# A two-column product of zeros ahead of a weight panel's run, and a dilated attention whose norm follows its first panel

## The reference

```python
def rms_norm(x, g):
    return x * lax.rsqrt(jnp.mean(x * x, axis=-1, keepdims=True) + EPS) * g

def swiglu(h, w_gate_up, w_down):                       # d_ff 2816
    gate, up = jnp.split(h @ w_gate_up, 2, axis=-1)
    return (jax.nn.silu(gate) * up) @ w_down

def first_block(x, ...):
    for i in range(4):                                  # fourier, s5, dilated, fourier
        x = x + mixer[i](rms_norm(x, norm_mix_g[i]))
        x = x + swiglu(rms_norm(x, norm_ffn_g[i]), ffn_w_gate_up[i], ffn_w_down[i])

def dilated_attention_mixer(h, w_qkv, q_gain, k_gain, w_o, rel_bias):
    qkv = (h @ w_qkv).reshape(b, s, 3, 3, 16, 64)       # 3 groups, (q, k, v), 16 heads
    for g, (window, dil) in enumerate(DILATED_GROUPS):
        q = head_rms_norm(qkv[:, :, g, 0], q_gain[g])   # t * rsqrt(mean(t * t) + EPS) * gain
        k = head_rms_norm(qkv[:, :, g, 1], k_gain[g])
        o, l = dilated_group_attention(q, k, qkv[:, :, g, 2], ...)
    ...                                                 # softmax over groups by l, then @ w_o

def second_block(x, ...):
    for i in range(2):
        h = h + 0.5 * swiglu_ffn(rmsnorm(h, norm_ffn1[i]), ...)
        u = rmsnorm(h, norm_mix[i]) @ w_mix_in[i]
        z, xbc, dt, q, k, v, q_idx, k_idx, w_idx = jnp.split(u, SPLIT_POINTS, axis=-1)
        h = h + jnp.concatenate([ssd_mixer(z, xbc, dt, ...), dsa_mixer(q, k, v, ...)], axis=-1) @ w_mix_out[i]
        h = h + 0.5 * swiglu_ffn(rmsnorm(h, norm_ffn2[i]), ...)
    return rmsnorm(h, final_norm)
```

## Time and profile before

| | |
|---|---|
| median of three executions | 2635.28 us |
| the profiled execution, own time | 2638.81 us |
| its span, first to last instruction | 2637.0 us |
| mean granted clock of TensorE | 0.982 |
| PE, PEld, DVE, ACT, POOL busy | 96%, 94%, 68%, 47%, 8% |
| products of panels | 18528, 48 for each of 386 panels |
| read from HBM | 426.45 MB, 162 GB/s over the span |

### The profile page before, as it was taken

The page is one execution under the profiler, slowest core; times in us unless marked ns, Lnnn a source line. Parts: engine busy times, 40 slices in busy tenths (PEclk is TensorE's granted clock), DMA queues, the critical chain, the costliest instruction groups (busy, mean ns, idle before and its releaser), DMA issues.

```text
span 2637.0 us, 54521 instructions
## 1 busy us (share of the span) xinstructions
PE 2526.9 (96%) x23166; PEld 2469.3 (94%) x23166; DVE 1783.4 (68%) x2299; ACT 1251.6 (47%) x1468; POOL 213.4 (8%) x246
## 2 busy tenths in 40 slices
PE   8999669999999899999999999999999999999998
PEld 7999669998999889999999999999999998999998
DVE  5988956565555665656666568976566557986655
ACT  5444434334566553344344346565334335665433
POOL 5000240003000100000000000600000000320000
PEclk9999889999999899999999999999999999999999
DMA  5553024555677735534545544434555554434553
GB/s 211 192 189 109 18 82 174 179 188 173 176 173 174 172 129 179 187 135 177 189 171 196 188 159 160 145 134 173 181 188 178 189 190 149 150 137 154 182 183 120
DMA packets 65839, 430.76 MB, mean 163 GB/s; under 512 B 8288, under 2 KB 11360, under 8 KB 15904
## 3 DMA queue, kind: packets, MB, share of 16 engines
q1 hardware_dynamic: 58864, 410.30, 43.3%
q0 software_dynamic: 6000, 17.46, 4.6%
q10 hardware_dynamic: 832, 0.92, 0.1%
HBM read 426.45 MB, written 1.15 MB: 162 GB/s over the span
## 4 chain that ended last, share of the span: by engine, by line
PE 88%; DVE 7%; ACT 3%; issue 1%; DMA 0%; DVEq 0%; ACTq 0%
PE psum L1989 26%; PE psum L1991 26%; PE psum L1990 26%; DVE w_lo L1313 1%; ACT w_hi L841 1%; PE psum L2022 1%; PE psum L2185 1%; PE psum L2091 1%; PE psum L2332 1%; PE psum L2320 1%; PE psum L2310 1%; PE psum L2276 0%; DVE h L1346 0%; PE psum L2074 0%; DVE rstd L1338 0%
## 5 line engine op out<-in xcount | busy, mean ns | idle before, releaser
L1989 PE MATMUL psum<-h_hi,w_hi 128*128 128x256 f32 x4320 | 1220.0, 282 | 20.9 <-DVE h_lo L1351 15.0
L1991 PE MATMUL psum<-h_hi,w_lo 128*128 128x256 f32 x4320 | 1211.2, 280 | 0.0
L1990 PE MATMUL psum<-h_lo,w_hi 128*128 128x256 f32 x4320 | 1210.6, 280 | 0.0
L841 ACT ACTIVATE w_hi<-raw 128x2048 fp32r<-128x2048 f32 x387 | 740.7, 1914 | 885.2 <-PE psum L1991 885.2
L1313 DVE TENSOR_TENSOR w_lo<-raw,w_hi 128x2048 fp32r<-128x2048 f32 x387 | 886.5, 2291 | 392.6 <-ACT w_hi L841 392.4
L1989 PEld LDWEIGHTS psum<-h_hi,w_hi 128*128 128x128 f32 x4320 | 814.8, 189 | 30.4 <-issue 25.7
L1990 PEld LDWEIGHTS psum<-h_lo,w_hi 128*128 128x128 f32 x4320 | 816.0, 189 | 0.7 <-issue 0.5
L1991 PEld LDWEIGHTS psum<-h_hi,w_lo 128*128 128x128 f32 x4320 | 815.5, 189 | 0.0
L1989 PE MATMUL psum<-act_hi,w_hi 128*128 128x256 f32 x1536 | 430.0, 280 | 0.7 <-DVE act_lo L1869 0.7
L1991 PE MATMUL psum<-act_hi,w_lo 128*128 128x256 f32 x1536 | 429.3, 280 | 0.0
L1990 PE MATMUL psum<-act_lo,w_hi 128*128 128x256 f32 x1536 | 428.9, 279 | 0.0
(11 more groups left out here) (329 smaller groups left out, 2374.3 us busy)
## 6 DMA issues: line engine op xcount, KB each, us to landing
raw<-in_panels SPq DMA_DIRECT2D x387, 1024.0 KB, 4.8
arena<-bias_by_distance POOLq DMA_DIRECT2D x32, 384.0 KB, 6.4
x<-in_x SPq DMA_DIRECT2D x1, 1024.0 KB, 5.7
arena<-in_s_cbd POOLq DMA_DIRECT2D x4, 256.0 KB, 3.0
arena<-in_s_b SPq DMA_DIRECT2D x1, 1024.0 KB, 15.2
arena<-in_s_c SPq DMA_DIRECT2D x1, 1024.0 KB, 17.1
hidden<-in_s_cbd POOLq DMA_DIRECT2D x4, 256.0 KB, 3.0
arena<-arena POOLq DMA_DIRECT2D x32, 32.0 KB, 1.9
```

Of the source, the lines that this page charges most:

```text
L841: a.activation(w_hi[:, s, :], raw[:, s, :], ACT.Copy).then_inc(hi_ready, 1)
L1989: t.matmul(o, w[0], xin[0], start=start, stop=False, skip_group_check=True)
L1990: t.matmul(o, w[0], xin[1], start=False, stop=False, skip_group_check=True)
L1991: return t.matmul(o, w[1], xin[0], start=False, stop=stop, skip_group_check=True)
```

## The change

It does three things.

The first is a new function, `lead`: one fp32 product of a 128 by 128 tile of zeros by two of its columns, into the first two columns of the bank that the coming panel clears as it starts. It stands behind the panel's wait for `lo_ready` and ahead of its first product. It is called 97 times: in the eight FFNs ahead of panel 1; in the two fourier mixers and in the S5 mixer ahead of the second panel; 32 times in dilated attention, ahead of each panel that stands behind another product; and 27 times in each mixer of the second network.

```diff
+            def lead(o, start=True):
+                z = zeros[:, :].bitcast(F32)
+                t.matmul(o[:, 0:2], z, z[:, 0:2], start=start, stop=True, skip_group_check=True)
...
-            def project(n, j, i=None, per=0, parts=None, o=None, frees=False):
+            def project(n, j, i=None, per=0, parts=None, o=None, frees=False, led=False):
...
+                    if led and k + m == 0:
+                        lead(o)
...
-                project(n0 + 1, 1)
+                project(n0 + 1, 1, led=True)
...
-            def project_tokens(n, o, tokens):
+            def project_tokens(n, o, tokens, led=False):
                 t.wait_ge(lo_ready, n + 1)
+                if led:
+                    lead(o)
...
+                def inner(p):
+                    return p >= 0 and 2 <= da_panel(p)[1] <= QK + 1
...
-                def arrive(p):
+                def arrive(p, led=False):
...
+                    led = p == Z + 3 or p == V + 1 or len(UNITS_AFTER[p - 1]) > 0
```

```diff
-            st["late"] = kind == "norm" and todo[len(stages) + 1][0] == "ffn"
+            st["late"] = kind == "norm" and todo[len(stages) + 1][0] in ("ffn", "dilated")
+            st["cols"] = kind == "norm" and todo[len(stages) + 1][0] == "dilated"
...
-                        a.activation(da.v[:, hb % 2, i - QK], b[:, :].rearrange("p (m n) -> p m n", m=2),
-                                     ACT.Copy).then_inc(v_copied, 1)
+                        for m in range(2):
+                            ins = a.activation(da.v[:, hb % 2, i - QK, m], b[:, m * S:(m + 1) * S], ACT.Copy,
+                                               scale=da.rstd[:, m:m + 1])
+                        ins.then_inc(v_copied, 1)
...
+                        if c == 0:
+                            a.wait_ge(rstd_ready, st["hn"] + 1)
+                        for qt in range(2):
+                            ins = a.activation(rq[:, :, qt], ss_q[:, :, qt], ACT.Sqrt, bias=da.eps[:, 0, qt:qt + 1])
+                        ins.then_inc(qk_rms_ready, 1)
...
+                if st["cols"]:
+                    for w, e in enumerate((E * EPS, EPS)):
+                        v.tensor_scalar(da.eps[:, w], bank[SUMS_BANK[True]][:, 0:2], e / D, e * EPS, ALU.mult, ALU.add)
+                    v.reciprocal(da.rstd, da.rstd).then_inc(rstd_ready, 1)
+                    return
...
-                t.wait_ge(rms_ready, st["hn"] + 1)
-                t.wait_ge(e_loaded, 16 * 5)
                 for p in range(PANELS):
-                    panel(p)
+                    panel(p, p == 1 or inner(p - 1))
+                    if p == 0:
+                        t.wait_ge(sq_added, 3 * (st["hn"] - st["whole"]))
+                        for qt in range(2):
+                            last = t.matmul(bank[SUMS_BANK[True]][:, qt:qt + 1], h[:, 0, qt::2], ones[:, 0:1],
+                                            start=True, stop=True)
+                        last.then_inc(ss_ready, 1)
+                t.wait_ge(rstd_ready, st["hn"] + 1)
```

More of the change, by code:

```diff
@@ L459, in build @@
         da.rk = da.take(2 * UNITS).rearrange("p (b n) -> p b n", b=2)
-        da.take(2 * 2 * S - 2 * UNITS)
+        da.rstd = da.take(2)
+        da.eps = da.take(2 * 2).rearrange("p (w t) -> p w t", w=2)
+        da.take(2 * 2 * S - 2 * UNITS - 6)
         da.rq = da.take(2 * NG * UNITS).rearrange("p (b g m t e) -> p b g m t e", b=2, g=NG, m=2, t=2)
@@ L873, in norm @@
                 a.wait_ge(ss_ready, n + 1)
-                a.activation(rstd[:, :], bank[SUMS_BANK[st["late"]]][:, 0:S], ACT.Sqrt, bias=eps[:, 0:1],
+                root, sums = (da.rstd, slice(0, 2)) if st["cols"] else (rstd[:, :], slice(0, S))
+                a.activation(root, bank[SUMS_BANK[st["late"]]][:, sums], ACT.Sqrt, bias=eps[:, 0:1],
                              scale=1.0 / D).then_inc(rms_ready, 1)
@@ L2279, in widen, with panel @@
                     last.then_inc(qk_wide_ready, 1)
-                def panel(p):
+                def inner(p):
+                    return p >= 0 and 2 <= da_panel(p)[1] <= QK + 1
+                def panel(p, led):
                     hb, i, _ = da_panel(p)
@@ L2340, in output @@
                     t.wait_ge(o_lo_ready, (tiles[-1] + 2) // 2)
+                    if k == 0 and tiles[0]:
+                        lead(bank[k], False)
                     for c in tiles:
@@ L2356, in dilated_mixer @@
                         scores(u)
-                    for p in da_panels(u):
-                        panel(p)
+                    for k, p in enumerate(da_panels(u)):
+                        panel(p, k == 0 or inner(p - 1))
                     if u and u % 2 == 0:
@@ L2384, in arrive, with accumulate @@
                     if p >= V:
-                        project_tokens(n0 + p, bank[p % PROJ_BANKS], (slice(0, P), slice(P, S)))
+                        project_tokens(n0 + p, bank[p % PROJ_BANKS], (slice(0, P), slice(P, S)), led=led)
                     else:
-                        project(n0 + p, p, parts=(h_lo_ready, 4 * st["hs"]) if p == 0 else None)
-                def accumulate(p, k, tile, tiles=range(KT)):
+                        project(n0 + p, p, parts=(h_lo_ready, 4 * st["hs"]) if p == 0 else None, led=led)
+                def accumulate(p, k, tile, tiles=range(KT), led=False):
                     t.wait_ge(lo_ready, n0 + p + 1)
+                    if led:
+                        lead(bank[k], p < OUT_ATT)
                     for c in tiles:
@@ L2480, in mixer @@
                 for half in range(2):
-                    arrive(Q + half)
+                    arrive(Q + half, led=True)
                     if half == 0:
@@ L2523, in mixer @@
                             t.wait_ge(y_lo_ready, 4 * i + b + 1)
-                            accumulate(p, 0, ssd_out_tile, (2 * b, 2 * b + 1))
+                            accumulate(p, 0, ssd_out_tile, (2 * b, 2 * b + 1), led and b == 0)
                     else:
-                        accumulate(p, p - OUT_SSD, ssd_out_tile)
+                        accumulate(p, p - OUT_SSD, ssd_out_tile, led=led)
                     for u in UNITS_AFTER[p]:
```

42 lines of the change are left out of this document (25 added, 17 removed).

## The result

Six executions of the changed kernel took 2646.86 us in the median (2644.95 to 2653.42), against 2635.53 (2633.09 to 2640.78) for six of the kernel before: the ratio is 1.0043, with a 95% interval of 1.0027 to 1.0059. The change made the kernel 11 us, 0.43%, slower. The forecast was 2580 us, with 2562 to 2640 as its range. The time is near the third rival's 2650: the leads cost what they were put at and did not make the long runs faster.

What follows compares the result with a forecast made beforehand. PE's step from product to product was taken as the bound: -74.9 us from faster runs, +21.3 for leads, -6.2 for norm and halves, is -59.8; 5 taken back leaves -55, so 2580 us by the median, range 2562 to 2640.

Steps and rivals of the forecast that it cites:

- the third rival: Leads leave every pace unchanged and cost 21.3 us, less 6.2 of the norm: +15.1, 2650 us; chance 0.18.
- The bound: In the FFNs PE is busy throughout at full clock; 18,528 products decide the time by the distance between starts.
- the terms: For the eight FFN runs, 12,384 products by 4.45 ns give 55.1 us, 6.9 us a run.
- If a lead puts the run behind it at 113.3 ns: All 97 places: runs behind leads go from 117.8 to 113.3 ns, together 74.9 us; main case, chance 0.53.
- the first rival: The pace is hit by chance, perhaps three FFN runs in eight catch: -12.2 us, 2623 us; chance 0.23.
- The leads' price: Each lead adds 0.22 us to PE's stream; 97 leads cost 21.3 us (7 to 39).
- the working's own warning: 86 leads outside FFN, fourier and S5 cost 18.9 us and may give 16.6.
- The norm and the halves: In dilated attention, the late norm and the halved roots and v copies together: -6.2 us (-8 to -2).
- The halves: Halved roots at dilated attention's widen step: six PE waits lengthen by 0.3 us each, 1.8 us in all.
- The norm's 19.2 us: Dilated attention's start, to the third panel's end, takes 19.2 us instead of 27.4, with no clock below 1.00.
- DVE as the bound: Leads work, but DVE holds back the first FFN entirely and seven others by 1 us each: 2589 us; chance 0.06.
- fewer than three of eight: The kernel gets slower wherever fewer than three of eight FFN runs catch the fast pace: (21.3 - 6.2) / 6.9 = 2.2.

Runs made afterwards that it cites:

- Experiment 6: Changed kernel without leads; in each FFN's panel 1 two fp32 zero products behind the fourth triple, one behind the tenth, in the bank half in use: 2579.27 us.
- experiment 1: Changed kernel with its 97 leads taken out and nothing else: 2631.46 us, ratio to before 0.9974.
- 3: Changed kernel without leads; two fp32 zero products behind panel 1's fourth triple, one behind the tenth, always written to the bank's first half: 2579.27 us, ratio 0.9774.
- 4: Changed kernel without leads; fp32 zero products in panel 1, pairs behind the third and seventh triple, one behind the eleventh, written to the bank's first half: 2583.60 us.
- 7: Experiment 6 with one fp32r zero product in place of the pair of fp32 products: 2578.94 us, ratio to before 0.9776.
- 9: Changed kernel without leads; one fp32 zero product behind the sixth triple of panel 1 in each FFN: 2617.51 us, ratio to before 0.9911.
- experiment 10: Experiment 6 with the change's 86 leads of dilated attention and the two mixers put back: 2599.26 us, ratio to before 0.9853.
- experiment 11: Kernel before with only experiment 6's two groups of zero products in panel 1 of each FFN: 2585.52 us, ratio to before 0.9804.
- 12: Changed kernel without leads; fp32r and fp32 zero products inside panel 1 of FFNs and S5, one fp32 ahead of the second panel in both second-network mixers: 2579.64 us.
- 2: Changed kernel with leads, plus zero products ahead of every FFN panel but its first, another form in each FFN: 2712.25 us in one execution.
- 5: Changed kernel without leads; ahead of FFN panels from 2 on, one fp32 zero product and another group alternately: 2672.42 us in one execution.
- 8: Changed kernel without leads; three fp32 zero products ahead of the first triple of panel 1 in each FFN: 2616.42 us, ratio 0.9914.

## Why the prediction was wrong

**The bound, right.** PE's step from product to product decides, with nothing late in an FFN. Experiment 6 shows the worth: the runs at 113.3 instead of 117.8 ns took 52 us off experiment 1's time, where the terms give 55.1 less 5.3 for the groups, 49.8; by the profiles it is 6.0 us in each of eight FFNs, the group's price already off.

**The step that failed: "If a lead puts the run behind it at 113.3 ns".** The working treated that as one event for all 97 places and gave it 0.53. A lead doesn't set a pace; it moves a run from one alignment to another, and which one it reaches depends on where the run was. Behind a settled run that is fixed (A and B to fast, C to A, fast to B). Ahead of a run, behind other products and behind a wait for DVE, it is a draw, and that is where the change put nearly all leads. In the profile 0 of 8 FFN runs came out fast; before it was 0 of 8 too, and in experiment 1 1 of 8. Over the ten profiles with nothing ahead of the FFN runs (before, 1, 3, 4, 6, 7, 9 to 12) 4 of 80 began fast. The first rival had the draw, but with three of eight. The rows bore out less than that: 13 of 100 at 113.3, and all eight FFN runs slow behind one and the same product. The value that followed from them is one in eight or less, and with that the first rival too would have ended above before's time. Nor is it an even draw: where the two mixers of the second network are the same, five of their places were fast in both, in the profile before. That one form is seen at two paces was read as a sign that a lead can choose; it was a sign of a draw.

**The leads' price, right.** 0.22 us was taken; the rows of experiment 6 give 0.22, experiment 10 gives 0.23 to 0.25, and 97 together cost 18 us (experiment 1) where 21.3 was forecast. The prediction had them hidden nowhere but in waits for `lo_ready`; six also lay in waits at the widen step, 1.3 us. The comparison of 0.22 for a lead with 0.214 that a panel of 48 can give back was the working's own warning that 86 of the 97 could not pay even if each worked.

**The norm and the halves, right in sum.** 6.2 us was forecast; experiment 11 gives 6.2 to 8, experiment 1 gives 6.9 (4.5 to 9.2). The halves cost what was forecast: in every profile with them and without leads in dilated attention PE waits 4.3 us at the widen step, 1.8 more than before. The norm's 19.2 us hang on the clock. It stayed at 1.00 behind the wait in six profiles (1, 2, 4, 5, 6, 9), and there the third panel ended 19.1 to 19.7 us after the FFN. In the changed kernel's profile and in those of 8 and 10 it was at half for 3.4 us, and the stretch took 21.0 to 21.3; in those of 3, 7 and 12 for 6.8 us, and it took 22.6. The forecast allowed for no such fall, and no run here shows what decides it: the wait was 1.75 us in the changed kernel and in experiment 1 alike.

**DVE as the bound, wrong.** In the densest stretch PE was never late, so nothing of the first FFN's 6.9 us is lost.

**The third rival, right but for its condition.** It priced a kernel in which no pace changes at 2650; measured were 2647. It argued that nothing touches the pace, and that is not so; that its sum came out near is in part luck. Nor do runs keep their pace over every wait in them, as it says and as the working has it for all 100. In the profile before, the output panels of dilated attention are one run with waits in it, and behind the last of these its pace changed:

```profile
953.61 0.28 PE L1989 MATMUL psum<-h_hi,w_hi 128*128 128x256 f32 x1
...
954.20 0.28 PE L1991 MATMUL psum<-h_hi,w_lo 128*128 128x256 f32 x1
955.03 0.35 PE L1989 MATMUL psum<-h_hi,w_hi 128*128 128x256 f32 x1 [0.56 <-DVE h_lo L1321]
955.23 0.28 PE L1990 MATMUL psum<-h_lo,w_hi 128*128 128x256 f32 x1
...
960.44 0.28 PE L1991 MATMUL psum<-h_hi,w_lo 128*128 128x256 f32 x1
```

0.59 us for five steps is 0.118; 5.21 for 46 is 0.1133. So the trace of before already held a pace that changed at a wait. The rival's rule "fewer than three of eight" was the right one.

**The rule for the gap.** The Trainium skill, "TensorE: Matmul & The Clock Gate", section "Back-to-back issue gap", gives N / 2.4 + 2.5 ns at full clock as the gap of an isolated product of N columns, 109 ns for 256. It says that this is not the spacing in a stream of weight loads and products, which both set, and has about 81 ns for 128 columns and 131 for 512 there. For a stream it has one spacing for a width. That is not borne out here: the same products ran at 113.3 or 117.8 ns, by what stood inside their run.

What stays open is why alignments exist at all, that is, what on the chip steps in 6.67 ns; why a draw behind three products has better odds than behind one, if it has; why some places begin in the same alignment again and again (six of eight in C); and whether the short panels could be led from one alignment to the fast one by a change that costs nothing, such as another order of the products already there. None of these was tried.

## What to carry to other kernels

Where one form of product shows two paces in a trace, count how often each appears and what stood before it; if places with the same predecessor differ, or one place differs between executions, it is a draw, and a step put ahead of it is only another draw. Try the step inside a settled run, away from waits, and tabulate state before and state after: here two small groups of zero products per FFN, 0.66 us, took all eight runs to the fast pace in each profile, 2.3% of the kernel. Then compare the price of a step with what its run can give back: 0.22 us pays over 1536 products and not over 48.

## What the runs showed of the hardware

- Triples of fp32r products, 128 columns loaded and 256 streamed, take 340.0, 353.3 or 360.0 ns, all multiples of 6.67 ns. In the FFNs they keep that over 1536 products, through loops and across panels; behind a wait inside a run it can change (0.118 to 0.1133 us behind 0.56 us, in the profile before).
- Two fp32 products of two columns, or one fp32r product of two columns, bring every slow alignment seen (A, B, C) to A or B; one fp32 product then brings A or B to the fast pace. One fp32 product did so 197 times of 197, and undid it 16 times of 16.
- A group that adds zeros must stay in the half of the bank that is being summed: written into the other half, behind that bank's newer start flag, it made the kernel's result wrong (experiments 3 and 4 against 6). By the Trainium skill, "PSUM — Partial Sum Buffer", section "The four PSUM rules", a starting product clears the written marks of its whole bank and the next adding product overwrites there, and the experiments agree.
- A wait of 1.75 us on PE was followed by 2.0 us at a granted clock of 0.50 and 1.7 us at 0.71 in the changed kernel's profile, and by a clock of 1.00 in that of experiment 1.
